# Two transformer blocks on one core: gate projections as eight half tiles inside the sparse attention, norm statistics earlier, rotations later

## The chip, the cores and the metric

One core of a Trainium2 chip runs the whole program. The metric is the device time of one execution in microseconds. Engines are named as in the profile: PE (TensorE), DVE (VectorE), ACT (ScalarE), POOL (GpSimd) and SP (SyncE, which only issues transfers here).

## What is computed

The reference is two blocks over x of 512 tokens by 1024 channels, all in float32. The first block is the one that the change touches:

```python
mod = silu(c) @ w_ada + b_ada                      # shift, scale, gate
h = rms_norm(x, norm_g) * (1 + scale) + shift
ssm_u, ssm_z, q, k, v, attn_z, q_idx, k_idx, w_idx = split(h @ w_in)
y_ssm  = s5_mixer(ssm_u, ...) * silu(ssm_z)        # diagonal state space model, gelu, glu gate
y_attn = dsa_mixer(q, k, v, q_idx, k_idx, w_idx, ...) * silu(attn_z)
x = x + gate * (concat([y_ssm, y_attn]) @ w_out)
# dsa_mixer: score[q, s] = sum_h w_idx[q, h] * relu(q_idx[q, h] . k_idx[s]), causal;
#            the 128 best keys of each query stay; softmax over them with a position bias; times v
```

The second block (retention, gated linear attention, window attention, their merge, a feed-forward network) follows it and is the same in both kernels.

## The kernel before

**Tiles and stages.** Every weight matrix is cut into tiles of 256 columns (up to 1 MB) in the order of the list STAGES, which is also the order in which SP loads them, into three slots of w_raw. A tile is split in two for the matmuls: ACT casts w_hi (`split_high`, two slots), DVE subtracts it for w_lo (`split_low`); activations are split likewise into h_hi and h_lo, or y_hi and y_lo. A product is hi x hi + lo x hi + hi x lo, so that one half tile (128 output channels by 512 tokens, `gemm_half`) is 24 matmuls. `ahead(gr)` splits the tile that follows group gr. Results go to three PSUM banks in turn, which ACT or DVE must free.

**Order.** There is no scheduler: each engine has its instructions in the order written, with counting semaphores between them. A wait blocks everything behind it on its engine.

**Start.** Eight tiles of modulation weights (`ada_rows`) come first, and `turned` brings each pair of rows to columns. The squares of x go through two buffers from ACT to PE (`stats_of("norm0")`, after the fourth tile), ACT takes the root, DVE the reciprocal (rstd), and DVE writes h in eight column tiles, two after each `modulation`. On ACT two sines stand behind the squares; on DVE the rest of the state space set-up stands behind the sines and ahead of rstd. `split_low(0)` follows the eight tiles.

**Index scores and selection.** `relevance` on PE gives 32 products, ACT's relu passes them through two buffers to DVE, which sums them into score. `select_keys(n)` does n rounds of eight maxima and their replacement; there are 48 rounds, 16 at each width of 256, 384 and 512. `rotations()` makes the tables cos_t and sin_t, about 90 small DVE instructions, ahead of the scores. `states(half)` runs the scan over the 64 chunks and needs these tables. The output rows of the state space model (`strip`) are made in four quarters on PE, each copied by ACT out of the same two banks; when all are there, DVE adds the diagonal (strip_ready) and POOL spreads them to toep with eight transfers.

**Gates.** The two tiles ssm_z are multiplied behind v, ahead of the state space output (y_psum), and ACT writes silu of them to sz. After the gelu come four ada_gate tiles and the glu; its tail on DVE (L1857 and L1858) multiplies the sigmoid with z32 and with sz and splits the result into y_hi and y_lo, and behind this `copied_dve` lets the attention begin. **Attention.** 32 items i (head i // 4, query tile i % 4, widths 128 to 512). PE does `logits(i + 2)`, `transposes(i)`, `values(i - 1)`; DVE does the reciprocal and the scaling of item i (p_norm), `masked_logits(i + 2)`, and after each eight items `attn_out`, which multiplies with az; ACT does the exponential of item i + 1 and the copy pT of item i. After i = 2, 10, 18 and 26 (AZ_AT) PE also does one half tile of attn_z, whose silu ACT writes to az at the same i.

## Time and profile before

| | us |
|---|---|
| median of three runs (lowest, highest) | 1789.53 (1789.14, 1791.19) |
| the profiled execution | 1785.86 |
| its span | 1783.8 |
| PE, DVE, ACT, POOL busy | 1635.9, 843.0, 592.0, 23.1 |
| mean granted clock of PE | 0.947 |

The span is from the first to the last instruction of the core; 2.06 us of the execution lie around it. A granted clock of 1.00 is 2.4 GHz, one of 0.50 is 1.2 GHz. In a timeline row the first number is the start, the second the length; the bracket at the end is the idle time of that engine just before the row, and what ended it.

### The profile page before, as it was taken

How to read it: one execution, taken by the hardware profiler on the slowest of the kernel's cores; microseconds unless marked ns; L12 is line 12 of the kernel's file. 1: busy time of each engine (PE TensorE's matmuls, PEld its weight loads, DVE VectorE, ACT ScalarE, POOL GpSimd, SP SyncE). 2: the span in 40 equal slices, each digit the busy share in tenths (PEclk: the TensorE clock that was granted, in tenths of full speed). 3: DMA queues.
4: the chain of work that ended last, by engine and by line, in shares of the span. 5: the costliest groups of instructions: out<-in, count | busy, mean ns of one | idle time of the engine just before them, and what ended most of it. 6: DMA issues, size and time to landing. Idle time of an engine off the chain costs nothing.

```text
span 1783.8 us, 19408 instructions
## 1 busy us (share of the span) xinstructions
PE 1635.9 (92%) x7920; PEld 1260.5 (71%) x7920; DVE 843.0 (47%) x1346; ACT 592.0 (33%) x855; POOL 23.1 (1%) x34
## 2 busy tenths in 40 slices
PE   6796989889898898999999999999998899999995
PEld 2474668545576676777778888788875588888874
DVE  2886678554435365534354454463343633333223
ACT  2233321444323254432243543333232322222221
POOL 0001010000000000000000000000000000000000
PEclk9898899967799999999999999999999899999998
DMA  7313142400223211112122212212231122222321
GB/s 296 118 72 94 49 75 71 166 0 1 85 107 116 95 48 48 48 72 71 49 94 102 95 71 71 71 71 94 95 142 71 47 95 95 95 95 89 109 86 47
DMA packets 23271, 152.25 MB, mean 85 GB/s; under 512 B 3328, under 2 KB 3888, under 8 KB 6912
## 3 DMA queue, kind: packets, MB, share of 16 engines
q1 hardware_dynamic: 20720, 137.43, 21.6%
q0 software_dynamic: 2464, 13.59, 2.8%
q8 instruction: 63, 1.03, 0.2%
q14 instruction: 24, 0.20, 0.0%
HBM read 144.55 MB, written 7.88 MB: 85 GB/s over the span
## 4 chain that ended last, share of the span: by engine, by line
PE 81%; DVE 11%; ACT 4%; issue 3%; DMA 1%; SPq 0%; ACTq 0%; DVEq 0%
PE bank L487 80%; DMA w_raw<-wstream 1%; ACT w_hi L1039 1%; DVE rstd L1570 1%; DVE w_lo L1550 1%; ACT lg L1329 1%; DVE tmp L1507 1%; PE bank L780 1%; DVE sv L1507 1%; DVE sgb L1514 1%; DVE tval L1581 1%; DVE h_lo L1565 1%; DVE lg L2017 0%; PE bank L845 0%; DVE sqb L1879 0%
## 5 line engine op out<-in xcount | busy, mean ns | idle before, releaser
L487 PE MATMUL bank<-h_hi,w_hi 128*128 128x512 f32 x1160 | 468.2, 404 | 30.3 <-DVE h_lo L1565 18.1
L487 PE MATMUL bank<-h_lo,w_hi 128*128 128x512 f32 x1160 | 458.6, 395 | 0.0
L487 PE MATMUL bank<-h_hi,w_lo 128*128 128x512 f32 x1160 | 457.6, 395 | 0.0
L1550 DVE TENSOR_TENSOR w_lo<-w_raw,w_hi 128x2048 fp32r<-128x2048 f32 (+2 forms) x114 | 256.7, 2254 | 363.0 <-ACT w_hi L1039 361.6
L487 PEld LDWEIGHTS bank<-h_hi,w_hi 128*128 128x128 f32 x1160 | 221.4, 191 | 93.7 <-issue 27.7
L1039 ACT CAST w_hi<-w_raw 128x2048 fp32r<-128x2048 f32 (+2 forms) x114 | 213.6, 1875 | 193.4 <-PE bank L487 184.0
L487 PEld LDWEIGHTS bank<-h_hi,w_lo 128*128 128x128 f32 x1160 | 221.2, 191 | 48.4
L487 PEld LDWEIGHTS bank<-h_lo,w_hi 128*128 128x128 f32 x1160 | 221.8, 191 | 46.8 <-issue 1.7
L487 PE MATMUL bank<-y_hi,w_hi 128*128 128x512 f32 x272 | 112.3, 413 | 3.4 <-issue 3.4
L487 PE MATMUL bank<-w_hi,h_hi 128*128 128x256 f32 x352 | 103.6, 294 | 3.6 <-DVE w_lo L1550 3.6
L487 PE MATMUL bank<-y_hi,w_lo 128*128 128x512 f32 x272 | 106.6, 392 | 0.0
L487 PE MATMUL bank<-y_lo,w_hi 128*128 128x512 f32 x272 | 106.4, 391 | 0.0
L487 PE MATMUL bank<-w_lo,h_hi 128*128 128x256 f32 x352 | 101.6, 289 | 0.0
L487 PE MATMUL bank<-w_hi,h_lo 128*128 128x256 f32 x352 | 101.4, 288 | 0.0
L1290 ACT ACTIVATE sgb<-bank 128x512 f32<-128x512 f32 x40 | 23.9, 598 | 168.9 <-PE bank L487 168.9
L487 PEld LDWEIGHTS bank<-w_hi,h_hi 128*128 128x128 f32 x352 | 69.6, 198 | 13.1 <-issue 13.1
L487 PEld LDWEIGHTS bank<-w_lo,h_hi 128*128 128x128 f32 x352 | 69.7, 198 | 0.0
L487 PEld LDWEIGHTS bank<-w_hi,h_lo 128*128 128x128 f32 x352 | 69.6, 198 | 0.0
L487 PE MATMUL bank<-f_hi,w_hi 128*128 128x512 f32 x176 | 69.3, 394 | 0.0
L487 PE MATMUL bank<-f_hi,w_lo 128*128 128x512 f32 x176 | 68.5, 389 | 0.0
L487 PE MATMUL bank<-f_lo,w_hi 128*128 128x512 f32 x176 | 68.5, 389 | 0.0
L487 PE MATMUL bank<-sqb,ones 128*128 128x512 f32 x112 | 56.0, 632 | 9.1 <-ACT sqb L1053 9.1
(320 smaller groups left out, 1836.0 us busy)
## 6 DMA issues: line engine op xcount, KB each, us to landing
w_raw<-wstream SPq DMA_DIRECT2D x120, 1024.0 KB, 4.8
xr<-xT SPq DMA_DIRECT2D x2, 2048.0 KB, 7.8
w_raw<-wstream SPq DMA_DIRECT2D x4, 768.0 KB, 4.2
bias_rows<-bias_table POOLq DMA_DIRECT2D x1, 2560.0 KB, 13.6
bias<-bias_rows POOLq DMA_DIRECT2D x1, 2048.0 KB, 8.9
x_saved<-xr POOLq DMA_DIRECT2D x1, 2048.0 KB, 9.7
xr<-x_saved POOLq DMA_DIRECT2D x1, 2048.0 KB, 8.1
outT<-down SPq DMA_DIRECT2D x8, 256.0 KB, 2.0
```

The lines of the kernel that those rows point to most:

```text
L487: return pe.matmul(out, lhsT, rhs, start=start, stop=stop)
L780: ins = pe.transpose(bank[PT_BANKS[i % 2]][:, s * P:s * P + P], prob(i, qt)[:, s * P:s * P + P], ident)
L1039: act.copy(w_hi[:, s % 2, 0:kt, :], w_raw[:, i % RAW_SLOTS, 0:kt, :]).then_inc(w_high, 1)
L1290: act.activation(sgb[:, m % 2, :], bank[bk][:, :], func).then_inc(bank_free[bk], 1)
L1329: ins = act.activation(lg[:, n % 2, j, 0:w], lg[:, n % 2, j, 0:w], ACT.Exp, bias=sst[:, 1, c + j:c + j + 1], accum_out=sst[:, 2, c + j:c + ...
L1507: settle(dve.tensor_tensor(out, a, b, op))
L1514: settle(dve.scalar_tensor_tensor(out=out, in0=a, scalar=s, in1=b, op0=op0, op1=op1))
L1550: dve.tensor_tensor(w_low_of(s)[:, 0:kt, :], w_raw[:, i % RAW_SLOTS, 0:kt, :], w_hi[:, s % 2, 0:kt, :].bitcast(f32), ALU.subtract).then_in ...
L1565: dve.tensor_tensor(dst, tval[:, a % 2, :] if src is None else src, hi.bitcast(f32), ALU.subtract).then_inc(act_low, 1)
L1570: dve.reciprocal(rstd[:, :], root[:, :]).then_inc(rstd_ready, 1)
L1581: dve.scalar_tensor_tensor(out=t, in0=src[:, m, :], scalar=gain(m), in1=rstd[:, :], op0=ALU.mult, op1=ALU.mult).then_inc(act_val, 1)
```

## The change

- The eight statistics matmuls run four behind the first modulation tile and four behind the second; the root follows the first copy of rows. `split_low(0)` moves up behind the sixth column tile, and `split_high(0)` behind the sixth h_hi.
- `rotations()` moves from ahead of the index scores to behind them, with tval as its scratch. `cl_ready` no longer waits for it. The two rounds of selection that stood there go.
- The strips' quarters are interleaved with the half tiles of k and v. Both calls of `states` now follow each other, and the diagonal comes behind them and behind three rounds of selection.
- ssm_z leaves its place. Its two tiles and those of attn_z become four groups of one tile, attn_z0, ssm_z0, attn_z1, ssm_z1, of which a half tile each stands behind i = 1, 2, 9, 10, 17, 18, 25 and 26 of the attention (GATE_FILL). ACT writes both silu of a tile at i = 3, 11, 19 and 27; the tiles are split ahead at i = 0, 8, 16 and 24.
- The glu's tail only writes sigmoid times z back to z32. The multiplication with sz and the split into y_hi and y_lo are at i = 12 and 28, two tiles each. y_ssm and y_attn share one numbering, y_at.

```diff
+        GATE_FILL = {1: ("attn_z0", 0), 2: ("attn_z0", 1), 9: ("ssm_z0", 0), 10: ("ssm_z0", 1),
+                     17: ("attn_z1", 0), 18: ("attn_z1", 1), 25: ("ssm_z1", 0), 26: ("ssm_z1", 1)}
...
-                if i == 3:
-                    stats_of("norm0", ones[:, :], 0, 8)
+                if i == 0:
+                    stats_of("norm0", ones[:, :], 0, 4)
+                if i == 1:
+                    stats_of("norm0", ones[:, :], 4, 8)
...
+            pe.wait_ge(cl_ready, 1)
+            pe.wait_ge(x_act, 4)
+            output_strip(0)
             gr = G["k"][1]
             gemm_half(gr, 0, "fm", h_hi, h_lo)
             key_stats(1)
+            output_strip(1)
             gemm_half(gr, 1, "fm", h_hi, h_lo)
             key_stats(2)
+            output_strip(2)
             gemm_half(G["v"][0], 0, "tm", h_hi, h_lo)
             key_stats(3)
+            output_strip(3)
             gemm_half(G["v"][0], 1, "tm", h_hi, h_lo)
...
-            for gr in G["ssm_z"]:
-                gemm(gr, "fm", h_hi, h_lo)
...
-                if i in AZ_AT:
-                    n = AZ_AT[i]
-                    gemm_half(G["attn_z"][n // 2], n % 2, "fm", h_hi, h_lo)
+                if i in GATE_FILL:
+                    name, half = GATE_FILL[i]
+                    gemm_half(G[name][0], half, "fm", h_hi, h_lo)
...
+                if i in (0, 8, 16, 24):
+                    ahead(G[GATE_FILL[i + 1][0]][0])
+                if i in (12, 28):
+                    for m in (0, 1) if i == 12 else (2, 3):
+                        high(y_at(m), y_hi[:, m, :])
+                if i - 1 in GATE_FILL and GATE_FILL[i - 1][1]:
+                    name = GATE_FILL[i - 1][0]
+                    gr = G[name][0]
+                    for half in range(2):
+                        bk = pbanks(gr)[half]
+                        act.wait_ge(group_done, 2 * gr.g + half + 1)
+                        settle(act.activation((az if name[0] == "a" else sz)[:, 2 * int(name[-1]) + half, :],
+                                              bank[bk][:, :], ACT.Silu))
...
+                if i == 2:
+                    split_low(0)
             input_low(7)
-            split_low(0)
...
             split_low(5)
-            rotations()
             dve.nop().then_inc(cl_ready, 1)
...
-            select_keys(2)
+            rotations()
...
+            split_low(8)
             states(0)
-            split_low(8)
+            states(1)
+            settle(dve.memset(ga_[:, :, 0:1], 0.0))
+            dve.memset(gb_[:, :, 0:1], 0.0).then_inc(state_ready, 1)
+            split_low(9)
+            select_keys(3)
             dve.wait_ge(strip_act, 8)
...
-            states(1)
-            settle(dve.memset(ga_[:, :, 0:1], 0.0))
-            dve.memset(gb_[:, :, 0:1], 0.0).then_inc(state_ready, 1)
-            split_low(9)
-            select_keys(5)
...
-            split_low(11)
-            select_keys(7)
-            split_low(12)
             select_keys(48)
...
-                    tt(sgb[:, m % 2, :], sgb[:, m % 2, :], z32[:, m, :], ALU.mult)
-                    a = AT["y_ssm"] + m
-                    dve.tensor_tensor(new_val(a), sgb[:, m % 2, :], sz[:, m, :], ALU.mult).then_inc(act_val, 1)
-                    dve.wait_ge(act_val, a + 1)
+                    tt(z32[:, m, :], sgb[:, m % 2, :], z32[:, m, :], ALU.mult)
                     dve.nop().then_inc(sig_used, 1)
-                for half in range(2):
-                    m = 2 * w + half
-                    low(AT["y_ssm"] + m, y_lo[:, m, :], y_hi[:, m, :])
...
+                if i in (12, 28):
+                    for m in (0, 1) if i == 12 else (2, 3):
+                        a = y_at(m)
+                        dve.wait_ge(az_ready, m // 2 * 4 + 4)
+                        dve.tensor_tensor(new_val(a), z32[:, m, :], sz[:, m, :], ALU.mult).then_inc(act_val, 1)
+                        low(a, y_lo[:, m, :], y_hi[:, m, :])
```

## Rows read from the trace of the kernel before

**Rows 1.** The page: busy engines, and the chain that ended last by engine.

```profile
PE 1635.9 (92%) x7920; PEld 1260.5 (71%) x7920; DVE 843.0 (47%) x1346; ACT 592.0 (33%) x855; POOL 23.1 (1%) x34
...
PE 81%; DVE 11%; ACT 4%; issue 3%; DMA 1%; SPq 0%; ACTq 0%; DVEq 0%
```

**Rows 2.** Stretches: from:to, length; busy PE, PEld, DVE, ACT, POOL; clock, DMA share, GB/s.

```profile
134.80:200.20 65.40, 48.18 (x178) 32.71 (x178) 37.38 (x95) 20.53 (x41) 8.79 (x9) 0.79 0.29 81
...
358.20:486.10 127.90, 109.05 (x400) 66.49 (x401) 62.05 (x202) 51.63 (x115) 0.00 (x0) 0.73 0.04 16
```

**Rows 3.** PE's waits from 134 to 245 us: total, times, longest.

```profile
PE bank L487 <- ACT sgb L1141: 17.1, 4, 13.1
PE bank L487 <- ACT strip L1177: 3.5, 3, 1.2
```

**Rows 4.** Table of stretches, in the attention behind one half tile.

```profile
383.40:400.70 17.30, 13.78 (x41) 7.39 (x38) 10.38 (x29) 5.20 (x15) 0.00 (x0) 0.50 0.00 0
374.70:383.40 8.70, 7.24 (x38) 4.19 (x38) 6.18 (x23) 5.76 (x14) 0.00 (x0) 1.00 0.01 2
```

**Rows 5.** Timeline of PE behind the same half tile.

```profile
378.06 1.09 PE L487 MATMUL bank<-pT,v 128*64 128x128 f32 x8
...
382.50 0.55 PE L780 MATMUL bank<-cst,sqb 128*128 128x128 f32 x3 [1.15 <-DVE sqb L1905]
...
386.08 1.11 PE L780 MATMUL bank<-cst,sqb 128*128 128x128 f32 x4 [1.20 <-DVE sqb L1905]
...
390.57 1.97 PE L487 MATMUL bank<-pT,v 128*64 128x128 f32 x8
...
397.11 0.66 PE L487 MATMUL bank<-pT,v 128*64 128x128 f32 x2 [1.94 <-DVEq L1896]
```

**Rows 6.** Timelines of ACT, DVE and PE in the first stage.

```profile
40.75 0.20 ACT L1080 ACTIVATE sv<-sv 128x16 f32<-128x16 f32 x1
...
52.34 3.35 DVE L1570 RECIPROCAL rstd<-root 128x512 f32<-128x512 f32 x1
...
68.84 4.49 DVE L1550 TENSOR_TENSOR w_lo<-w_raw,w_hi 128x2048 fp32r<-128x2048 f32 x2
...
71.17 0.79 PE L487 MATMUL bank<-h_hi,w_hi 128*128 128x512 f32 x1 [11.32 <-DVE w_lo L1550]
```

**Rows 7.** Table of stretches, DVE at line 1507 alone: the rotations, one states.

```profile
128.80:153.05 24.25, 20.99 (x87) 0.82 0.51 131
...
211.20:222.90 11.70, 8.25 (x12) 1.00 0.26 91
```

**Rows 8.** Timeline of DVE: the mask behind the index scores.

```profile
201.42 4.10 DVE L1510 TENSOR_SCALAR score<-cst 128x128 f32<-128x128 f32 x1
```

**Rows 9.** Stretches: ssm_z; five selection rounds at 256; sixteen at 512.

```profile
276.90:298.80 21.90, 21.90 (x100) 17.86 (x98) 18.19 (x42) 5.57 (x6) 0.00 (x0) 1.00 0.28 97
245.60:250.50 4.90, 4.63 (x26) 4.66 (x27) 4.59 (x16) 0.00 (x0) 0.00 (x0) 0.65 0.75 220
...
300.00:324.30 24.30, 23.15 (x229) 15.74 (x230) 23.18 (x49) 9.64 (x17) 0.90 (x1) 1.00 0.30 108
```

**Rows 10.** Timeline of PE: the first logits.

```profile
358.21 0.55 PE L487 MATMUL bank<-k,q 64*128 64x128 f32 x1 [6.19 <-DVEq L1868]
```

**Rows 11.** Timeline of ACT at the first half tile of attn_z.

```profile
367.54 1.90 ACT L1039 CAST w_hi<-w_raw 128x2048 fp32r<-128x2048 f32 x1
...
374.67 0.60 ACT L1264 ACTIVATE az<-bank 128x512 f32<-128x512 f32 x1 [3.93 <-PE bank L487]
375.44 1.28 ACT L1241 ACT_TABLE_LOAD   x1 [0.17 <-ACT az L1264]
376.74 0.40 ACT L1241 ACTIVATE sgb<-sgb,stat 128x128 f32<-128x128 f32 x1
```

**Rows 12.** Timeline of DVE in attn_out.

```profile
396.21 0.69 DVE L1893 TENSOR_TENSOR tval<-bank,az 128x512 f32<-128x512 f32 x1
397.59 0.69 DVE L1565 TENSOR_TENSOR y_lo<-tval,y_hi 128x512 fp32r<-128x512 f32 x1 [0.68 <-ACT y_hi L1047]
```

More of the change, by code:

```diff
@@ L71 @@
     ("v", _cols("w_in", 2048, 512)),
-    ("ssm_z", _cols("w_in", 512, 512)),
     ("ada_gate", _cols("w_ada", 2048, 1024)),
     ("glu", _cols("w_glu", 0, 512, kt=4)),
-    ("attn_z", _cols("w_in", 2560, 512)),
+    ("attn_z0", _cols("w_in", 2560, WC)),
+    ("ssm_z0", _cols("w_in", 512, WC)),
+    ("attn_z1", _cols("w_in", 2560 + WC, WC)),
+    ("ssm_z1", _cols("w_in", 512 + WC, WC)),
     ("out1", _cols("w_out", 0, 1024)),
@@ L116, with y_at @@
     _at += _n
+Y_ORDER = [4, 0, 1, 5, 6, 2, 3, 7]
+def y_at(m):
+    return AT["y"] + Y_ORDER.index(m)
 class Group:
@@ L697, in _, with output_strip @@
             key_stats(0)
-            pe.wait_ge(cl_ready, 1)
-            pe.wait_ge(x_act, 4)
-            for q in range(4):
+            def output_strip(q):
                 if q:
@@ L1091, in _ @@
                 act.copy(mrow[0:1, i * SEQ:(i + 1) * SEQ], bank[4 + i][0:1, :]).then_inc(mod_row, 1)
-                if i == 1:
+                if i == 0:
                     root_of("norm0", D)
@@ L1095, in _ @@
                     input_high(2 * i - 4, 2 * i - 2)
+            input_high(4, 6)
             split_high(0)
-            input_high(4, 8)
+            input_high(6, 8)
             def evacuate(gr, half, dst, scale=1.0):
@@ L1173, in _, with strip_copy @@
             head_chunk("k", 1, k32)
-            for q in range(4):
+            def strip_copy(q):
                 act.wait_ge(strip_psum, q + 1)
@@ L1178, in _ @@
                              bank[5 + r][0:GCH, :].rearrange("p (i c) -> p i c", c=P)).then_inc(strip_act, 1)
+            strip_copy(0)
             ahead(G["k"][1])
             head_chunk("k", 2, k32)
+            strip_copy(1)
             head_chunk("k", 3, k32)
+            strip_copy(2)
+            ahead(G["v"][0])
+            strip_copy(3)
             act.wait_ge(sq_used, SQ0["k"] + 4)
@@ L1186, in _ @@
             for w, gr in enumerate(G["v"]):
-                ahead(gr)
+                if w == 0:
+                    evacuate_tm(gr, 0, v32[:, 0:2, 0:WC])
+                    evacuate_tm(gr, 1, v32[:, 2:4, 0:WC])
+                    continue
                 for half in range(2):
@@ L1190, in _ @@
             act.nop().then_inc(copied_act, 2)
-            act.wait_ge(state_ready, 1)
-            for w, gr in enumerate(G["ssm_z"]):
-                if w == 0:
-                    ahead(gr)
-                for half in range(2):
-                    act.wait_ge(group_done, 2 * gr.g + half + 1)
-                    bk = pbanks(gr)[half]
-                    settle(act.activation(sz[:, 2 * w + half, :], bank[bk][:, :], ACT.Silu))
-                    act.nop().then_inc(bank_free[bk], 1)
             for q in range(4):
@@ L1232, in _ @@
                     act.nop().then_inc(bank_free[bk], 1)
-                for half in range(2):
-                    m = 2 * w + half
-                    high(AT["y_ssm"] + m, y_hi[:, m, :])
             def probabilities(i):
@@ L1255, in _ @@
                 if i >= 8 and i % 8 == 1:
-                    high(AT["y_attn"] + i // 8 - 1, y_hi[:, 3 + i // 8, :])
-                if i in AZ_AT:
-                    n = AZ_AT[i]
-                    gr, half = G["attn_z"][n // 2], n % 2
-                    if half == 0:
-                        ahead(gr)
-                    bk = pbanks(gr)[half]
-                    act.wait_ge(group_done, 2 * gr.g + half + 1)
-                    settle(act.activation(az[:, n, :], bank[bk][:, :], ACT.Silu))
-                    act.nop().then_inc(az_ready, 1)
-                    act.nop().then_inc(bank_free[bk], 1)
-            high(AT["y_attn"] + 3, y_hi[:, 7, :])
+                    high(y_at(3 + i // 8), y_hi[:, 3 + i // 8, :])
+                if i in (0, 8, 16, 24):
[11 more added lines that the diff above has]
+                                              bank[bk][:, :], ACT.Silu))
+                        act.nop().then_inc(az_ready, 1)
+                        act.nop().then_inc(bank_free[bk], 1)
+            high(y_at(7), y_hi[:, 7, :])
             for w, gr in enumerate(G["out1"]):
@@ L1849, in _ @@
                 low(AT["z"] + m, y_lo[:, 4 + m, :], y_hi[:, 4 + m, :], z32[:, m, :])
-            split_low(13)
+            split_low(G["glu"][0].s)
             for w, gr in enumerate(G["glu"]):
@@ L1855, in _ @@
                     dve.wait_ge(sig_ready, m + 1)
-                    tt(sgb[:, m % 2, :], sgb[:, m % 2, :], z32[:, m, :], ALU.mult)
-                    a = AT["y_ssm"] + m
-                    dve.tensor_tensor(new_val(a), sgb[:, m % 2, :], sz[:, m, :], ALU.mult).then_inc(act_val, 1)
-                    dve.wait_ge(act_val, a + 1)
+                    tt(z32[:, m, :], sgb[:, m % 2, :], z32[:, m, :], ALU.mult)
                     dve.nop().then_inc(sig_used, 1)
-                for half in range(2):
-                    m = 2 * w + half
-                    low(AT["y_ssm"] + m, y_lo[:, m, :], y_hi[:, m, :])
             dve.wait_ge(ada_done, 6)
@@ L1910, in _ @@
                     attn_out(i - 2)
-                if i == 6:
-                    ahead(G["attn_z"][0])
-                if i == 22:
-                    ahead(G["attn_z"][1])
+                if i in (0, 8, 16, 24):
+                    ahead(G[GATE_FILL[i + 1][0]][0])
+                if i in (12, 28):
[4 more added lines that the diff above has]
+                        low(a, y_lo[:, m, :], y_hi[:, m, :])
             attn_out(31)
```

13 lines of the change are left out of this document (6 added, 7 removed).

## The prediction

> **What bounds the kernel now.** I read the page first, then a table of stretches, then PE's idle rows, then the timeline of each engine. TensorE (PE) is busy 92% of the span and carries 81% of the chain of work that ended last [rows 1]. So the question for each edit is whether PE has less to do, waits less, or gets a higher clock. The table of stretches shows where the kernel is weak: from 134.8 to 200.2 us, and in the sparse attention, 127.9 us long, where PE is busy 109 us of it at a mean granted clock of 0.73 [rows 2]. The index stage waits 13.1 us in one piece [rows 3]. The attention is a chain over four engines (logits on PE, bias and maximum on DVE, exponential on ACT, scaling on DVE, transpose on PE, copy on ACT, values on PE). Only four half tiles of the gate projection lie in it. After each, the clock is 2.4 GHz (granted 1.00) for 8.7 us, then 1.2 GHz (0.50) for 17.3 us [rows 4], and in that slow part the idle pieces before PE are all under 2 us [rows 5]: there PE itself, at half speed, is the bound. The same eight value matmuls take 1.09 us in the fast part and 1.97 in the slow one [rows 5].
>
> I walk the new order through these stages; times are microseconds from the start of the span.
>
> **Norm statistics and the first low half.** Before, the eight statistics matmul pairs run after four modulation tiles, so ACT's two sines start only at 40.75, the DVE set-up behind them follows, and 1/rms starts at 52.34; DVE then writes h_lo to 68.9 and the two low halves of weights to 73.3, and PE idles 11.3 us until 71.17 [rows 6]. After, the statistics end some 7.5 us earlier (PE does two tiles, 7.2 us, after them instead), 1/rms starts about 45, and DVE is then paced by the last modulation rows: they come at about 57.5 (PE's work is the same, less its 1.6 us of idle between tiles). The last two column pairs cost DVE 3.3 us each in the old trace. With w_lo of the first tile (2.3 us) placed between them, and its cast (1.9) behind the sixth h_hi on ACT, I get w_lo ready at 65.0 and the last h_lo at 69. PE can begin at 65.0: its first 15 matmuls at 1.2 GHz (0.43 us each) stay behind h_lo. Gain 6.2 us. Bounds 1.5 (DVE's stall at the new split costs what it gives) to 7.
>
> **Rotations.** They take DVE 24.25 us [rows 7], in front of the index scores, and cause the 13.1 us wait on PE [rows 3]. Moved behind the scores this wait goes, with about 1.6 us of half clock after it. So PE's first half tile of k starts at 200.2-20.9 = 179.3. But the rotations still run on DVE, now ahead of the low half of the second k tile. DVE ends the scores at 180.5 and then has, without a gap: the 4.1 us mask, which stands beside POOL's memset [rows 8]; 24.25 rotations; 0.4; 2.3 for w_lo: 211.7. PE, through its 17.6 us of other work and one strip, is ready at 199: it waits 12.9 us. **The wait is moved, not removed.** Then states twice, 11.7 each [rows 7] with two memsets, and w_lo again, 2.3 (4.49 for two, [rows 6]): 237.7, where PE waits a second time, some 6.7 us, ahead of v. The strips by quarters save three waits of 1.16 us on PE, but PE isn't last here. They cost something: the fourth strip now stands behind the first half of v (7.6 to 8.1 us after such a wait), a statistics matmul and its own 1.9, so DVE, which has done three selection rounds, waits at the strips until 249.9. Then 1.4 for the diagonal, 3.35 for the reciprocal (as of the same width in [rows 6]), 2.2 for w_lo, four rounds and 2.7 for k: 263.6.
>
> The Trainium skill ("SBUF — State Buffer", Who interferes with whom) says that a DVE instruction with two SBUF inputs contends only with a GpSimd instruction that reads SBUF, not with one that writes. By it the rotations wouldn't suffer from the memset, whose remaining part is covered by the mask anyway. No time in my sum hangs on it.
>
> **ssm_z leaves.** PE loses 21.9 us here [rows 9], so the y phase starts at about 271.3 (its other condition, the toeplitz rows, at about 267), 27.5 early, and the gate rows end at 310.8. But DVE has 41 of the 48 selection rounds to go where it had 30 at the old 277: nine at 0.98 and sixteen at 1.52 [rows 9], and sixteen of the width between at 1.25, with their marks 54.4 us in all: 318. Then 2.5 for the low halves of z and 1.2 for w_lo: the glu matmuls start at about 321.7, not 339.45, with PE idle 10.9 us and cold (about 1 us more): gain 16.8 at their end. **Selection becomes the bound.** Bounds of the gain: 12 (each wait above 1 us longer, less in the head) and 20.
>
> **glu tail.** PE waits 6.19 us for the multiplications with silu(z) and their split [rows 10]; of that chain only a sigmoid (0.7), one multiplication (0.7) and 0.16 stay: about 2.0. Gain 4.2. The attention starts **21.0 us early**, bounds 15 to 25.
>
> **The attention.** Added, over what it has:
> - Four half tiles: 21.9/4 = 5.5 us [rows 9], with their surroundings 5.74 each: +23.0. They hide nothing: DVE waits for PE after each half tile already, being only two steps ahead.
> - Low halves split one item ahead at i = 0, 8, 16, 24: cast 1.9 [rows 11] and then 2.3 on DVE stand ahead of the scaling that the next transpose waits for. From the transpose: 0.3+1.9+2.3+0.5 = 5.2, against 3.6 to 4.0 of other PE work. At i = 0 +3.3, at the others +1.1; the two old ones cost 1.2 each [rows 5]: +4.2.
> - Both silu now stand at i = 3 behind the copy of pT, after the half tile has ended, where before the first table load was under it. ACT: 1.28+0.6+0.6+1.28 [rows 11] with settling 4.2 ahead of the next exponential. PE's slack to its next transpose is about 2.1, so 1.8, and the part of the fast stretch that goes idle is paid again at 1.2 GHz: 2.2 x 4 = +8.8. Bounds 0 and 4.2 each.
> - Gates at i = 12 and 28: DVE multiplies, waits for ACT's high half, subtracts, twice; 0.69+0.68+0.69 per tile by the like group of attn_out [rows 12], with queueing behind an exponential and a copy 5.5 in all, 3.9 over DVE's slack: 2 x 3.9 = +7.8. Bounds 0 and 5.5 each.
> - Given back: item i = 10 (and 18, 26) between two half tiles runs fast, -0.9 each, and the start is warm because PE idles 2 us and not 6: -1.6. Together -4.3.
>
> Sum +39.5; bounds +19 (only the half tiles and what is given back) and +48.
>
> The skill's "ScalarE: Activation LUTs", What ACT_TABLE_LOAD costs, gives some 2.7 us for a table load with its drain, and 1.28 for the instruction. The rows show 1.28 and the next activation 0.02 us behind it [rows 11], so I go by 1.28; by 2.7 each of the four blocks would be 2.8 us longer and the whole +11 us.
>
> Nothing behind the attention changes: out1 and its loads keep their order, and the y values are complete as before.
>
> **Sum.** -21.0+39.5 = +18.5 us. The profiled execution took 1785.86 us (span 1783.8, 2.06 around it), 3.7 under the median of the runs, 1789.53. 1785.9+18.5 = 1804.4 on its basis, **1808.0** on that of the median.
>
> **Rivals.**
> (a) *The clock stays at 2.4 GHz in the attention* (the side of faster): with twice the half tiles the 17.3 us at half clock go. DVE is busy 10.4 us there [rows 4], with one hand-over of 1.94 it takes 12.3: 5.0 less per round, 1.5 less in the half tile that begins cold, 6.5 x 4 = 26: 1782. It turns the result from 19 us on. For it: more dense work per round. Against: the fall comes 9 us after the end of a half tile, with nothing dense behind it, in all three rounds, and these 25 us of each round have no more dense work than before. 0.14.
> (b) *Silu, splits and gates lie beside PE at half clock*: then the attention grows by 18.7 only, -21.0+18.7: 1787, no difference. For it: DVE and ACT are busy 62 and 52 of 127.9 us [rows 2]. Against: they stand in the chain, and before the fall PE has waits already [rows 5]. 0.15.
> (c) *The waits make the clock fall one step sooner* and the front gives only 16: +8+5: 1821. For it: idle 1.8 us within the fast stretch. 0.16.
> (d) The change does as it says, as sketched: 0.55.
>
> **How the numbers follow.** About 0.2% (3.6 us) is what a measurement of this kernel can tell from no change. Faster: (a) and the lower part of (b): 0.17. Same: the rest of (b) and the low edge of (d): 0.13. Slower: 0.70. The range leaves out the far half of (a) and of (c): 1783 to 1820.
>
> **What would show it.** In the new profile: PE's first long matmul row near 65; no wait on the relu's buffers at the index scores; a wait for w_lo of some 13 us before the second k tile and one of 7 before v; glu near 321.7 behind the last selection; first logits near 337; the attention 167 us long, with the clock at 0.50 for 17 us between pairs of half tiles, and waits of 2 us at i = 5 and of 4 at i = 13 and 29. An attention under 150 us, or no half clock in it, makes me wrong.

## The result, and the profile after

| | us |
|---|---|
| before, median of four runs (lowest, highest) | 1790.36 (1789.14, 1792.47) |
| after, median of four runs (lowest, highest) | 1804.41 (1803.56, 1804.75) |
| ratio, 95% interval | 1.0075 (1.006, 1.009) |
| the profiled execution after, its span | 1804.35, 1802.5 |

The change costs 14.0 us by the medians, and 18.5 us from one profiled execution to the other. That these two differ is a result of its own, taken up below. One later execution of the kernel before took 3260 us and stands outside all the spreads that follow.

The page of the kernel after answers [rows 1]: PE's busy time has grown by 7.4 us without any more work for it, and its share of the chain that ended last fell from 81 to 78%, DVE's rose from 11 to 13.

```profile
PE 1643.3 (91%) x7920; PEld 1265.8 (70%) x7920; DVE 844.3 (47%) x1346; ACT 589.7 (33%) x854; POOL 23.1 (1%) x34
...
PE 78%; DVE 13%; ACT 5%; issue 3%; DMA 1%; SPq 0%; ACTq 0%; DVEq 0%
```

Its table of stretches, columns as in [rows 2]. The first stretch has the old one's bounds: PE busy 60.3 us for 48.2, at 0.90 for 0.79. The second runs from the first half tile of k to the y phase: PE is idle 20 of 94 us and DVE busy 78.7. The third is the attention, 165.8 us for 127.9.

```profile
134.80:200.20 65.40, 60.31 (x371) 42.84 (x372) 36.95 (x98) 25.34 (x48) 7.96 (x7) 0.90 0.24 67
181.10:275.20 94.10, 73.72 (x570) 59.88 (x570) 78.69 (x214) 19.81 (x30) 9.02 (x10) 0.84 0.23 47
338.50:504.30 165.80, 133.91 (x496) 85.91 (x497) 72.29 (x212) 59.34 (x125) 0.00 (x0) 0.74 0.09 34
```

PE's waits (total, times, longest) from 134 to 338 us answer [rows 3]: the 13.1 us on ACT's relu are gone, and a wait for w_lo stands there in three pieces.

```profile
PE bank L498 <- DVE w_lo L1572: 27.5, 3, 13.0
PE bank L498 <- ACT sgb L1160: 4.3, 4, 1.9
```

The three pieces, and the first logits, in PE's timeline (start, length, then in brackets the idle time before): the second tile of k, v, the glu, the attention's start, and out1 behind it.

```profile
213.54 0.76 PE L498 MATMUL bank<-h_hi,w_hi 128*128 128x512 f32 x1 [13.03 <-DVE w_lo L1572]
...
239.33 0.55 PE L498 MATMUL bank<-w_hi,h_hi 128*128 128x256 f32 x1 [6.79 <-DVE w_lo L1572]
...
323.87 0.77 PE L498 MATMUL bank<-y_hi,w_hi 128*128 128x512 f32 x1 [7.69 <-DVE w_lo L1572]
...
338.51 0.67 PE L498 MATMUL bank<-k,q 64*128 64x128 f32 x3 [2.01 <-DVEq L1881]
...
504.32 0.63 PE L498 MATMUL bank<-y_hi,w_hi 128*128 128x512 f32 x1 [2.21 <-issue]
```

So the attention began 19.7 us early and took 37.9 us longer. From out1 to the end of the span there are 1298.2 us, where the kernel before has 1297.7: nothing else changed. Inside the attention the clock shows what [rows 4] showed, with longer rounds: one pair of half tiles lies in the stretch at 1.00, and before and behind it PE runs at 0.50 for 20.5 and 23.9 us.

```profile
371.30:391.80 20.50, 17.42 (x47) 10.58 (x48) 10.39 (x28) 6.95 (x16) 0.00 (x0) 0.50 0.00 0
391.80:408.90 17.10, 15.59 (x72) 10.71 (x71) 4.82 (x17) 5.97 (x12) 0.00 (x0) 1.00 0.18 62
408.90:432.80 23.90, 17.30 (x48) 9.99 (x49) 14.60 (x38) 9.32 (x22) 0.00 (x0) 0.50 0.00 1
```

The waits in the attention are those that the prediction named, in the timeline of PE: behind the split of i = 0, behind the two silu, and behind the multiplications of i = 12.

```profile
346.91 0.69 PE L798 MATMUL bank<-cst,sgb 128*128 128x128 f32 x2 [2.94 <-DVE sgb L1918]
...
369.54 0.44 PE L798 MATMUL bank<-cst,sgb 128*128 128x128 f32 x2 [2.06 <-DVE sgb L1918]
...
412.69 0.69 PE L798 MATMUL bank<-cst,sgb 128*128 128x128 f32 x2 [5.30 <-DVE sgb L1918]
```

### The profile page after: what moved, and what is told of

Same layout as the page of the kernel before. It is cut to its first block, busy times and chain, and to the rows that moved or that the text cites. A ratio compares the mean times of both kernels' runs of the same rounds, so it can differ in the third digit from the quotient of the medians.

```text
span 1802.5 us, 19410 instructions
## 1 busy us (share of the span) xinstructions
PE 1643.3 (91%) x7920; PEld 1265.8 (70%) x7920; DVE 844.3 (47%) x1346; ACT 589.7 (33%) x854; POOL 23.1 (1%) x34
## 4 chain that ended last, share of the span: by engine, by line
PE 78%; DVE 13%; ACT 5%; issue 3%; DMA 1%; SPq 0%; ACTq 0%; DVEq 0%
PE bank L498 77%; DVE score L1788 2%; DVE small L1787 1%; ACT w_hi L1057 1%; DVE w_lo L1572 1%; ACT lg L1351 1%; PE bank L798 1%; DVE rstd L1592 1%; DVE tval L1529 1%; DVE lg L2034 1%; DVE sgb L1536 1%; DMA w_raw<-wstream 1%; DVE tval L1603 1%; DVE h_lo L1587 1%; DVE sv L1529 0%
## 5 line engine op out<-in xcount | busy, mean ns | idle before, releaser
L1312 ACT ACTIVATE sgb<-bank 128x512 f32<-128x512 f32 x40 | 23.9, 598 | 168.9 <-PE bank L498 168.9
L498 PEld LDWEIGHTS bank<-y_hi,w_hi 128*128 128x128 f32 x272 | 51.8, 191 | 23.2 <-issue 12.6
## 6 DMA issues: line engine op xcount, KB each, us to landing
bias_rows<-bias_table POOLq DMA_DIRECT2D x1, 2560.0 KB, 14.6
```

The lines of the kernel that those rows point to most:

```text
L498: return pe.matmul(out, lhsT, rhs, start=start, stop=stop)
L1312: act.activation(sgb[:, m % 2, :], bank[bk][:, :], func).then_inc(bank_free[bk], 1)
```

## The experiments

The theory: the front of the kernel gains only what DVE lets it gain, because the rotations moved within the same queue; the attention pays for the half tiles, and for whatever DVE and ACT do in its chain without a half tile beside it. The rivals: each part is worth its own stall; PE at half clock hides DVE and ACT; the clock alone decides. Every run is timed against the kernel before on the same chip; differences are between these medians unless a profile is named. The whole change was timed on its own, so a difference from it carries the intervals of both ratios, some 3 us together; what one edit is worth in the attention is therefore read from the attention's length in the profiles.

### The statistics alone

Only the first part of the change is made.

```diff
-                if i == 3:
-                    stats_of("norm0", ones[:, :], 0, 8)
+                if i == 0:
+                    stats_of("norm0", ones[:, :], 0, 4)
+                if i == 1:
+                    stats_of("norm0", ones[:, :], 4, 8)
```

> The kernel before with the first part of the change alone: statistics behind the first two modulation tiles, the first low half of weights behind the sixth column. Mine: the first k_idx matmul comes 5.8 us early, as in the profile of the kernel with the whole change (65.4 for 71.2); DVE's low halves behind it come 5.5 early too (109.4 for 114.9), so the rotations start earlier with them, the 13.1 us wait at the index scores stays what it was, and all behind it moves by 5.7: 1790.4-5.7 = 1784.7. Rival: the shift is lost at a transfer (the toeplitz rows, a weight tile) before the y phase: 1790. Rival: DVE is the bound from the start, and PE only waits longer for the rotations: 1788 or more.

Measured: 1781.81 us for 1789.61, ratio 0.9957 (0.9942 to 0.9973): 7.8 us faster, not 5.7. In the profile all shifts as expected: the waits of 13.1 us at the index scores and 3.6 ahead of v stay, and the glu starts 3.9 us early, at 335.60 for 339.45, with the first modulation tile landing 1.9 later (17.79 for 15.84).

```profile
PE bank L487 <- ACT sgb L1144: 17.1, 4, 13.1
PE bank L487 <- DVE w_lo L1553: 3.6, 1, 3.6
```

In this profile the first k_idx matmul starts at 66.60. The 2 us beyond the sum led to the next run.

### The kernel before once more

Nothing is changed. Its runs had lain between 1784 and 1794, while those of the kernel with the early statistics all lay between 1780.1 and 1782.5.

> The kernel before, unchanged, as its own control, for the profile of another execution. Its runs lay between 1784 and 1794, those of the kernels with the statistics behind the first two tiles within 1.5 of their median. Mine: the spread is the landing of the third and fourth modulation tile, for which PE waits before the statistics: 0.9 and 0.7 us in the profile of 1785.9, 4.3 in one of 1809.5 whose first k_idx matmul came 5.3 us later. So in this profile the waits there and the start of the first k_idx matmul (71.2 in the first profile) move with its time, one for one: 1790 goes with 75. Rival (the spread lies elsewhere, in transfers of the second block): the first k_idx matmul within 1 us of 71.2 at any time.

Measured: 1790.56 for 1789.99, ratio 0.9999 (0.9988 to 1.001), and the profiled execution took 1790.38. As expected, 1790 goes with a first k_idx matmul at 75. Its timeline of PE at the modulation tiles, and that matmul:

```profile
17.22 9.73 PE L487 MATMUL bank<-w_raw,silu_c 128*1 128x256 f32 x32 [9.45 <-DMA w_raw<-wstream]
30.06 8.44 PE L487 MATMUL bank<-w_raw,silu_c 128*1 128x256 f32 x32 [3.11 <-DMA w_raw<-wstream]
...
75.10 0.79 PE L487 MATMUL bank<-h_hi,w_hi 128*128 128x512 f32 x1 [11.32 <-DVE w_lo L1550]
```

The same rows of the first profile, taken at 1785.86 us, are:

```profile
15.84 9.89 PE L487 MATMUL bank<-w_raw,silu_c 128*1 128x256 f32 x32 [8.08 <-DMA w_raw<-wstream]
26.63 3.61 PE L487 MATMUL bank<-w_raw,silu_c 128*1 128x256 f32 x16 [0.90 <-DMA w_raw<-wstream]
30.95 3.61 PE L487 MATMUL bank<-w_raw,silu_c 128*1 128x256 f32 x16 [0.71 <-DMA w_raw<-wstream]
```

The tiles of weights landed later, PE waited 3.11 us for 1.61 behind the first two and began 1.4 later, the two tiles behind the wait took 8.44 us for 7.22, and all of it comes out at the end: the first k_idx matmul is 3.9 us later and the time 4.5 us longer. With the statistics behind the first two tiles PE has 7.7 us of work between the landings and waits for none but the first. So the start at 65.40 of the whole change is 5.8 us early against the first profile and 75.10-65.40 = 9.7 against this one, which lies at the median. With the statistics alone the start was 66.60, as the first tile landed later there: 8.5 early against this profile, where the medians gave 7.8.

### All that lies ahead of v, and the gates alone

The next two kernels split the change in two. First the statistics, the rotations, the strips and the order of the states, with ssm_z and the attention as before:

```diff
-            rotations()
             dve.nop().then_inc(cl_ready, 1)
...
-            select_keys(2)
+            rotations()
...
+            split_low(8)
             states(0)
-            split_low(8)
...
+            states(1)
```

> The kernel before with every part of the change ahead of v (statistics, rotations behind the scores, strips by quarters, order of the states and the diagonal), while ssm_z, its silu, the glu tail and the attention stay as before. Mine: the rotations take back what the index scores give. In the two profiles v ends at 277.0 before and at 275.2 with the whole change, so with ssm_z back behind v the y phase starts 1.8 us early, selection is hidden by ssm_z and the gate rows again, and the time is 1788.6: about 4 us slower than the statistics alone. Rival (the parts simply add, each by its own stall): 5.8 of the head and 13.1 of the wait less 13.0 and 3.2 of the new ones, 1787.7 to 1785. Rival of the sum on record, which put v's end 5.6 us early: 1784.8.

Measured: 1784.55 for 1789.61, ratio 0.9968 (0.9958 to 0.9978): 5.1 us faster, less than the statistics alone by 2.7 us. Against the kernel with the statistics alone the expectation was +3.9 us. Two stretches of this kernel, from the first k_idx matmul to the y phase and from there to the glu:

```profile
65.90:294.40 228.50, 202.07 (x1124) 155.98 (x1124) 166.27 (x331) 68.15 (x101) 17.78 (x19) 0.91 0.26 70
294.40:338.30 43.90, 40.22 (x306) 23.62 (x305) 33.14 (x70) 13.81 (x23) 0.90 (x1) 0.92 0.38 132
```

And of the kernel with the statistics alone:

```profile
66.60:294.90 228.30, 202.56 (x1124) 156.52 (x1124) 170.57 (x344) 68.35 (x101) 17.78 (x19) 0.91 0.25 70
294.90:335.60 40.70, 37.02 (x306) 22.39 (x305) 28.61 (x59) 13.68 (x23) 0.90 (x1) 1.00 0.42 143
```

Up to the y phase both take the same time, 228.5 and 228.3 us: the new waits for w_lo (20.3 us in two pieces) are as long as the old ones on relu, w_lo and strips (17.1, 3.6 and 3.5, less the 4.3 that stay on relu). The rotations behind the scores and the strips by quarters are worth nothing where PE is the bound behind them, as expected, but not for 3.9 us of a later v: the 3.2 us lie in the stretch behind, where the granted clock was 0.92 and not 1.00. What turned the clock down there isn't shown, and one profile of each doesn't tell whether it does so every time. That the absolute time came out at 1784.6 and not 1788.6 fits the late tiles again: this kernel, too, waits for none behind the first.

Then the gates' part alone:

```diff
-    ("ssm_z", _cols("w_in", 512, 512)),
...
+    ("attn_z0", _cols("w_in", 2560, WC)),
+    ("ssm_z0", _cols("w_in", 512, WC)),
...
-                    tt(sgb[:, m % 2, :], sgb[:, m % 2, :], z32[:, m, :], ALU.mult)
+                    tt(z32[:, m, :], sgb[:, m % 2, :], z32[:, m, :], ALU.mult)
```

> The kernel before with the gates' part alone: ssm_z into the attention as half tiles, silu, splits and multiplications there, the shorter glu tail; statistics, rotations and strips as before. Mine: selection is the bound of this stage whatever stands ahead of it. Before, DVE ends it at 324.7 with two low halves of ssm_z in between (4.6 us), which go: 320.1, where the whole change has 320.0. So the glu matmuls start at 323.9 +- 0.7, as in the whole change, the attention takes 165.8, and the time is that of the whole change, 1804.4 +- 1: the other parts are worth nothing there. Rival (each part is worth its share): without the 5.8 of the head and the shorter wait it is 6 us slower than the whole change, 1810.

Measured: 1807.65 for 1789.61, ratio 1.0098 (1.0079 to 1.0117), where the whole change has 1.0075 (1.006 to 1.009); its runs lie between 1804.4 and 1809.8. The median, 3.2 us above that of the whole change, lies between the two theories, and the intervals of the two overlap. The profiled execution, 1809.5, was one with late tiles:

```profile
31.15 8.75 PE L498 MATMUL bank<-w_raw,silu_c 128*1 128x256 f32 x32 [4.30 <-DMA w_raw<-wstream]
...
76.50 0.79 PE L498 MATMUL bank<-h_hi,w_hi 128*128 128x512 f32 x1 [11.32 <-DVE w_lo L1552]
...
328.38 0.47 PE L498 MATMUL bank<-y_hi,w_hi 128*128 128x512 f32 x1 [1.77 <-issue]
```

The first k_idx matmul is 5.3 us later than in the first profile of before. Taken off, the glu starts at 323.1, where the whole change has 323.87: with the tiles early, all the other parts together would be worth nothing beside the gates, as expected. PE is idle only 1.77 us there, for 7.69 in the whole change, so it is nearly as late as selection. That with late tiles the other parts are worth what the statistics save is argued from these two profiles, not measured.

### The rotations in the gaps

The whole change, with the rotations cut in four.

```diff
+            rot = rotations()
             for i in range(32):
+                if i in (3, 11, 19, 27):
+                    next(rot)
...
-            rotations()
             dve.wait_ge(root_ready, ROOT["q"] + 1)
```

> The whole change, with the rotations cut in four pieces that stand in DVE's idle gaps among the index scores (idle 2.6, 6.3, 6.3 and 10.0 us; pieces of 3.8, 6.1, 6.0 and 8.3) and not behind the scores. Mine: the 13.0 us wait for w_lo ahead of the second k tile goes, DVE ends everything behind it 16 to 18 us sooner, and as selection ends the stage, glu starts at 306 and not at 323.9: 1786.5. The 7 us wait ahead of v stays, since both states stand ahead of its low half. Rival (PE or a transfer is the bound once the wait is gone): gate rows end at 303 to 310, and the gain is 10 or less, 1795. Rival (the pieces run over in the gaps and hold up the scores): 6 us less gain, 1792.

Measured: 1782.70 for 1789.61, ratio 0.9964 (0.9952 to 0.9976), which is 20 us less than the whole change by the two ratios (21.7 by the medians), where 18 were expected. Both waits for w_lo ahead of v went, not only the first: v starts at 219.54 behind 0.55 us. PE's timeline at the y phase and at the glu:

```profile
250.59 0.43 PE L498 MATMUL bank<-cl_re,ga_ 64*64 64x128 f32 x4 [0.82 <-DMA toep<-strip]
...
301.29 0.76 PE L498 MATMUL bank<-y_hi,w_hi 128*128 128x512 f32 x1 [11.22 <-DVE w_lo L1572]
```

The glu starts 22.6 us sooner, and still PE waits 11.22 us for DVE there: selection is the bound of this stage, and 24 us taken out of DVE's queue come back nearly whole.

### What DVE and ACT do in the attention

Three kernels change one thing each. The splits of the gates' tiles beside the second half tile:

```diff
-                if i in (0, 8, 16, 24):
-                    ahead(G[GATE_FILL[i + 1][0]][0])
+                if i in (2, 10, 18, 26):
+                    ahead(G[GATE_FILL[i][0]][0])
```

> The whole change, with the casts and low halves of the gates' tiles made beside the second half tile of each pair (i = 2, 10, 18, 26), not one item ahead of the first (i = 0, 8, 16, 24). Mine: they cost because DVE's 2.3 and ACT's 1.9 stand in the chain from scaling to transpose; beside 5.7 us of matmuls they cost nothing. Of the waits in the profile of the change, 2.94 at i = 1 becomes 1.1, and 1.04 before the transpose and 1.69 before the values at i = 8, 16, 24 become about 1.0 together: 2 + 3 x 1.5 = 6.5 less, 1804.4-6.5 = 1798. Rival (PE at half clock covers them already, as the old kernel's splits were covered): 1803 or more. Rival (the tiles come too late to be loaded for the next pair): waits before i = 9, 17, 25, 1806.

Measured: 1796.91 for 1790.41, ratio 1.0039 (1.0027 to 1.0051): 7.5 us under the whole change (6.4 by the two ratios), where 6.5 were expected. The attention in its table of stretches:

```profile
339.60:499.90 160.30, 134.49 (x496) 86.51 (x497) 72.67 (x212) 59.54 (x125) 0.00 (x0) 0.76 0.10 36
```

The attention is 5.5 us shorter: idle time of PE fell from 31.9 to 25.8 us, its busy time stayed. Next, two of the four multiplications at i = 17:

```diff
-                if i in (12, 28):
+                if i in (17, 28):
```

> The whole change, with the first two of the four multiplications with silu(z), their high and low halves, at i = 17 beside a half tile and not at i = 12, where nothing covers them; those at i = 28 stay. Mine: the wait of 5.3 us before the transposes of i = 13 falls to about 1.4, like the same place without them, and beside the half tile of i = 17 (5.7 us, with the 2.7 of the attention's own output already there) 8.2 us of DVE stand, so 1.5 come back: 1804.4-2.4 = 1802. The 5.3 at i = 29 stays as the control. Rival (free at half clock, the wait is put down to them only): 1804.4. Rival (all of the 5.3 is theirs): 1799 to 1800.

Measured: 1800.68 for 1790.41, ratio 1.0058 (1.0045 to 1.007), 3.7 us less, where 2.4 were expected; by the times alone this isn't clear of noise. The profile shows it: the attention is 162.9 us long, 2.9 less. The 5.30 us became 2.06, and the one at i = 29 stayed:

```profile
410.34 0.69 PE L798 MATMUL bank<-cst,sgb 128*128 128x128 f32 x2 [2.06 <-DVE sgb L1918]
...
493.17 0.69 PE L798 MATMUL bank<-cst,sgb 128*128 128x128 f32 x2 [5.30 <-DVE sgb L1918]
```

And the gates' eight half tiles without silu:

```diff
-                                              bank[bk][:, :], ACT.Silu))
+                                              bank[bk][:, :], ACT.Copy))
```

> The whole change, with a plain copy in place of silu for the eight gate half tiles of the attention (this leaves silu out, so the values differ); the copies are as long, but the two table loads around each pair (1.28 us each) go. Mine: the block on ACT falls from 4.2 to 1.6 us, the 2.06 us wait before the transposes of i = 5, 13's follower and their like goes, and the clock falls later: the sum on record had 8.8 for four blocks, the larger part of which is table loads: 1804.4-6 = 1798. Rival (the loads lie beside PE at half clock or are hidden): 1804. Rival (a wait in the fast stretch costs more than its length, by the clock): 1794.

Measured: 1791.43 for 1789.99, ratio 1.0017 (1.0006 to 1.0028): 13 us less (10 by the two ratios), where 6 were expected. The attention, 10.8 us shorter:

```profile
339.50:494.50 155.00, 126.87 (x496) 82.88 (x497) 72.06 (x212) 49.23 (x117) 0.00 (x0) 0.80 0.10 39
```

ACT is busy 10.1 us less, the eight table loads at 1.26 each. PE's idle time fell by only 3.8 us, but its busy time by 7.0: the clock fell later (mean 0.80 for 0.74). The rival with the clock was right on the size: a wait in the stretch at 1.00 costs more than its length. Of the 13 us, 3 lie elsewhere: behind the attention this profile has 1295.1 us, that of the splits' kernel 1295.0, and those of all the others 1297.2 to 1298.2. Why isn't shown.

### The half tiles spread over the attention

The half tiles are spread, and with them move the splits (each beside a half tile) and the first two multiplications (to i = 17), as in the two kernels above.

```diff
+        GATE_FILL = {1: ("attn_z0", 0), 5: ("attn_z0", 1), 9: ("ssm_z0", 0), 13: ("ssm_z0", 1),
+                     17: ("attn_z1", 0), 20: ("attn_z1", 1), 23: ("ssm_z1", 0), 26: ("ssm_z1", 1)}
```

> The whole change, with the eight half tiles spread over the attention (i = 1, 5, 9, 13, 17, 20, 23, 26) and not in four pairs; silu behind the second of each tile, splits beside a half tile, the first two multiplications at i = 17. What is computed is the same. Mine: the clock is the price of this stage. After each half tile it is at 2.4 GHz for 8.7 us, and four items take some 8.5 us at it, so between i = 1 and i = 30 the half-clock stretches of 17 to 24 us all but go: eight blocks of 8.5 + 5.7, 4 us for the multiplications at i = 28 and 8 for the ends, 126 us for 165.8: 1764. Rival (the clock falls between single half tiles too, since only a pair keeps it up): only the splits and the multiplications get their cover, 1795. Rival (DVE's chain is the bound at full clock): items of 2.7 us, 140 us, 1779.

Measured: 1786.83 for 1790.41, ratio 0.998 (0.9972 to 0.9989): 17.6 us under the whole change, not 40, and enough to bring it below the kernel before. The attention is 18.5 us shorter, but 5.5 and 2.9 of this were had by the splits and the multiplications alone; if the three add, some 10 are left for the spreading. The attention, the first stretch in it at 1.00, and the one behind that:

```profile
340.20:487.50 147.30, 123.61 (x497) 80.93 (x497) 72.67 (x212) 59.98 (x125) 0.00 (x0) 0.83 0.10 38
...
350.80:374.70 23.90, 21.59 (x105) 14.51 (x104) 12.44 (x39) 11.88 (x24) 0.00 (x0) 1.00 0.13 45
374.70:384.90 10.20, 8.26 (x22) 4.96 (x21) 4.49 (x13) 2.45 (x7) 0.00 (x0) 0.50 0.00 0
```

The clock stayed up for 23.9 us across four items and a half tile, and then fell where PE had waited 2.31 us behind the two silu. So the rival that only a pair keeps it up falls, but the theory's 126 us fall too. The next kernel adds a front without waits for w_lo (rotations in the gaps, six rounds of selection ahead of the states, the third w_lo between the states):

```diff
             split_low(8)
+            select_keys(6)
             states(0)
+            split_low(9)
             states(1)
```

> The half tiles spread as in the run before this one, and the rotations in DVE's gaps among the index scores, with six rounds of selection ahead of the first states and the low half of the third tile of weights between the two states, so that neither of the waits for w_lo (13.0 and 6.8 us) is left. Mine: the two parts add, as they lie in different stages. Rotations in the gaps alone made glu start at 301.3; without the second wait, and with DVE never waiting for the strips, selection ends 8 us sooner: 293. 1804.4-22-8-40 = 1734. Rival (the y phase then waits for the toeplitz rows, which came 0.8 us late with the rotations in the gaps): selection goes on beside that wait, so no loss. Rival (the half tiles don't keep the clock): 1766.

Measured: 1762.72 for 1790.41, ratio 0.9846 (0.9833 to 0.9859), 27.7 us faster than before, but 29 behind what was expected: the attention is 147.1 us, like the 147.3, and glu starts at 298.81 and not 293, still behind 5.29 us of wait.

```profile
298.81 0.77 PE L498 MATMUL bank<-y_hi,w_hi 128*128 128x512 f32 x1 [5.29 <-DVE w_lo L1572]
```

Then every such step beside a half tile:

```diff
+        GATE_FILL = {1: ("attn_z0", 0), 4: ("attn_z0", 1), 8: ("ssm_z0", 0), 12: ("ssm_z0", 1),
+                     16: ("attn_z1", 0), 20: ("attn_z1", 1), 24: ("ssm_z1", 0), 27: ("ssm_z1", 1)}
+        SILU_AT = dict(zip((4, 8, 12, 16, 20, 24, 27, 28), GATE_FILL.values()))
+        GATE_AT = {16: 0, 24: 1, 30: 2}
```

> As the run with the half tiles spread and the rotations in the gaps, but with all that the gates ask of DVE and ACT beside a half tile: half tiles at i = 1, 4, 8, 12, 16, 20, 24, 27; one silu beside each following half tile and not two behind every second one; the attention's own output at i = 8, 16, 24 beside a half tile; the multiplications with silu(z) at i = 16, 24, 30 and behind the loop. Mine: in that run the clock fell three times at the same spots, where PE had waited 2.3 us behind the two silu and 1.9 us for the output's bank (half clock from 349.1 to 359.4, 383.3 to 393.5, 414.0 to 420.8). Without these waits it stays at 2.4 GHz from the first half tile to the last: 3 x (4.3 of waits + 4 of half clock) less, and 3 of the 5.3 us at i = 29: 1762.7-27 = 1736, the attention 120 us. Rival (the clock falls there anyway, waits or not): only the waits go, 1750. Rival (ACT is overloaded beside a half tile: 1.9 + 3.2 + 1.2 us of 5.7, the next scaling late): 1755 to 1762.

Measured: 1760.05 for 1789.99, ratio 0.9834 (0.9819 to 0.9849), the fastest of all by its median, though its interval overlaps the last one's. The mechanism failed: the attention was to take 120 us. The attention, two stretches in it, and the two waits in PE's timeline before the clock fell:

```profile
316.10:463.80 147.70, 134.15 (x497) 88.27 (x497) 72.38 (x212) 71.25 (x134) 0.00 (x0) 0.77 0.12 47
...
326.70:360.80 34.10, 31.81 (x151) 21.44 (x149) 18.11 (x57) 18.12 (x35) 0.00 (x0) 1.00 0.09 32
360.80:371.00 10.20, 10.20 (x31) 6.94 (x31) 5.48 (x13) 6.29 (x8) 0.00 (x0) 0.50 0.00 0
...
344.94 0.55 PE L800 MATMUL bank<-cst,sqb 128*128 128x128 f32 x3 [1.15 <-DVE sqb L1929]
...
359.24 0.55 PE L800 MATMUL bank<-cst,sqb 128*128 128x128 f32 x3 [1.15 <-DVE sqb L1929]
```

The long waits did go: PE is idle 13.5 us, where it was 23.6 in the run before and 31.9 in the whole change. Yet it is busy 10.7 us longer for the same matmuls, since the mean clock is 0.77 for 0.83. The clock stayed at 1.00 for 34 us and then fell 1.6 us behind a wait of only 1.15 us, where the same wait at 344.94 had no fall behind it. Waits of 1.15 us stayed every four items, and each of the six falls in this attention lies in such a wait or less than 2 us behind its end (the last in one of 1.83). So the short waits aren't ruled out as the cause: no kernel here is without them. What went out as idle time came back as half clock, and the attention takes 147.7 us for 147.1.

### ssm_z back in its place

The front of the last two, with the gates as in the kernel before. Against the two kernels before it, it has these lines back, among others.

```diff
+            for gr in G["ssm_z"]:
+                gemm(gr, "fm", h_hi, h_lo)
```

> Everything ahead of v as in the fastest front so far (statistics early, rotations in DVE's gaps, six rounds of selection ahead of the states, the third w_lo between them, strips by quarters), but the gates as in the kernel before: ssm_z behind v, four half tiles of attn_z in the attention, multiplications in the glu's tail. It asks what moving ssm_z into the attention is worth once DVE doesn't hold up the glu. Mine: nothing either way. Gate rows end 21.9 us later than with the half tiles spread (293.5 + 21.9 = 315.4), glu starts 1.2 behind, the wait before the first logits is 6.2 and not 2.0, the attention 127.9 us as before: out1 starts at 463 where that kernel has 461.9, so 1764, within 4 us of it. Rival (PE's wait for selection stays, or the toeplitz rows hold up the y phase): 1770. Rival (the attention with few half tiles is shorter than in the first profile, as its waits were 1.9 and 1.2 only): 1758.

Measured: 1764.76 for 1787.85, ratio 0.986 (0.9836 to 0.9883), as expected (1764), which can't be told from the kernel with the same front and the half tiles spread (0.9833 to 0.9859). Its six runs lie wide, between 1757.3 and 1769.1, and the profiled one took 1767.23. The attention, beside 127.9 us before:

```profile
338.40:467.10 128.70, 109.13 (x401) 67.01 (x401) 62.08 (x202) 51.58 (x115) 0.00 (x0) 0.73 0.04 16
```

The glu starts at 319.42, 1.21 us behind PE's work before it, as in the kernel before (1.21). Moving ssm_z is worth nothing that these runs can tell once DVE isn't in its way. In the whole change, where it is, moving it costs: the gates' part alone made the kernel 18 us slower.

## Why the prediction was right, point by point

The forecast was slower, at 1808.0 us; it is slower, at 1804.4, and within the range. By the profiled executions the sum came out exact (+18.5), and this is in part luck: the front gave 1.3 us less than forecast and the attention cost 1.6 less, and within the attention the silu was priced too low and the rest too high.

- **Norm statistics.** PE began at 65.40, forecast 65.0; 1/rms at 43.35, forecast about 45. Against the profile that was read, the term of 6.2 us measured 5.8. Against the median of the kernel before it is 9.7, and here the forecast erred: it took the profiled execution's 3.7 us below the median for scatter and added them to the sum. They were the landing of the modulation tiles, a wait that this edit removes. On the profiled execution's basis the forecast was 1804.4 and the profiled execution after took 1804.35. The sum of +18.5, less the 3.9 us by which the head is later at the median, gives +14.6; measured +14.0.
- **Rotations.** k began at 181.09, forecast 179.3, a gain of 19.1 for 20.9: 0.4 less from the head, and of the 1.6 us of half clock that were to go with the wait only 0.2 did (5.8 + 13.1 + 0.2). The wait was moved, not removed: 13.03 us, forecast 12.9, and 6.79, forecast 6.7.
- **ssm_z leaves.** The y phase began at 275.15, forecast 271.3, because v stood behind the strips and partly at half clock; the gate rows ended at 316.18, forecast 310.8. Both errors cost nothing, since selection was the bound, as the prediction said: glu at 323.87, forecast 321.7, behind 7.69 us of wait, forecast 10.9. Where DVE isn't the bound the same miss might count; no run tests it.
- **glu tail.** 2.01 us before the first logits, forecast 2.0. The attention started 19.7 us early, forecast 21.0.
- **Attention.** +37.9 us, forecast +39.5. The second half tile of each pair takes 5.67 us in PE's timeline (356.57 to 362.24 the first), 22.7 for the four beside 23.0. The waits were 2.94 at i = 1 (forecast +3.3 there), 2.06 behind silu (forecast 1.8), 5.30 at the multiplications (3.9 over the slack). The price of each, taken away alone and read from the attention's length, was 5.5 us for the four splits (forecast 3.3 + 3 x 1.1 = 6.6), 2.9 for one pair of multiplications (3.9), and 10.8 for the table loads of the silu alone, more than the 8.8 of the whole block. 5.5 + 2 x 2.9 + 10.8 = 22.1 for a forecast of 23.2; with the forecast's 23.0 for the half tiles, less its own 2.4 for the old splits and 4.3 given back, neither measured alone, 38.4, beside 37.9 measured. The mechanisms held, and so did their sum; the silu was priced too low, since a wait in the fast part takes clock with it, and the rest too high. The upper bound of this sum was added up wrongly: its own upper terms give 50.7 (23.0 + 4.2 + 16.8 + 11.0 - 4.3), not 48. That they add near this arrangement doesn't mean that they do elsewhere: see the last two kernels with spread half tiles.
- **The rivals.** (a), the clock stays up: no, 20.5 and 23.9 us at 0.50 in the first two rounds. Spreading the same half tiles raises the mean clock from 0.74 to 0.83, but doesn't keep it up either. (b), beside PE at half clock: no, PE's waits on DVE's scaling are 24.5 us in the attention, for 10.8 before, and each of the three parts, moved or taken away, made it shorter. (c), the clock falls sooner: 9.0, 6.7, 8.9 and 6.6 us behind the four pairs of half tiles, where it was 8.7 to 9.6 behind the first three half tiles of the kernel before, so clearly sooner in two rounds; its 8 us didn't show in the sum.

What stays open: what makes the clock fall in the attention. It fell behind waits of 2.3 us in one kernel and of 1.15 us in another, at nearly the same length of the attention, and it didn't fall behind a like wait of 1.15 us. No run here separates PE's idle time from the kind of matmuls that stand between two half tiles, and none takes out the short waits. The last kernel with spread half tiles also places them, the silu and the multiplications otherwise, so the idle time isn't all that changed.

## What to carry to other kernels

A step moved within one engine's queue moves its wait; cut in pieces that fit the engine's idle gaps, it went away (some 20 us here, for the same instructions). Before a median is set against a sum from one profiled execution, look where the two differ: if the difference is a wait that the change removes, it belongs in the sum. In a stage whose clock comes and goes, waits that were taken out can come back as half clock, so such a stage is to be measured in PE's busy time as well as in its waits.

## What the runs showed that had not been expected

- The spread of the kernel before, 1784 to 1794 us, comes at least in good part from the first 30 us: PE waited 1.6, 3.1 and 4.3 us for modulation tiles in three executions of the same code there, with the times 1785.9, 1790.4 and, with the gates' part, 1809.5. With 3.8 us of other matmuls behind each of the first two tiles the spread of the statistics' six runs was 2.4 us. That isn't all of it, though: of the kernels with the same start, the one with a copy for silu spread by 9.4 us over eleven runs and the one with ssm_z in its place by 11.8 over six, and for this no cause is shown.
- Half clock beside a fully busy PE: from 360.8 to 371.0 us PE was busy 10.20 of 10.20 us at a granted clock of 0.50, behind 34.1 us at 1.00 with 2.3 us idle in all. The clock was down for those 10.2 us although PE had no idle time in them; it came back in the half tile that began at 367.39.
- Halving PE's idle time in the attention, from 23.6 to 13.5 us, changed its length by 0.6 us, the wrong way.
